# Two attentions of a two-block transformer: half of the value evictions on VectorE, another PSUM bank for x at one border, and a new order of weight splits at the ends of both attentions

## The reference, cut to what matters

```
for layer in range(2):
    h = rms_norm(x, norm_mix_pre[layer])
    h = neighbourhood_attention(...) if layer == 0 else dilated_attention(...)
    x = x + rms_norm(h, norm_mix_post[layer])
    h = rms_norm(x, norm_ffn_pre[layer])
    x = x + rms_norm(swiglu(h, ...), norm_ffn_post[layer])
```

## Time and profile before

| | us |
|---|---|
| median of 3 executions | 1777.59 |
| lowest, highest | 1774.07, 1777.84 |
| the profiled execution: its time | 1775.63 |
| the profiled execution: span from first to last instruction | 1773.8 |
| PE busy | 1760.5 (99% of the span) |
| DVE busy | 1233.4 (70%) |
| ACT busy | 1000.0 (56%) |
| POOL busy | 97.4 (5%) |

### The profile page before, as it was taken

How to read it: one execution, slowest core, us unless ns; L and a number is a source line. 1 busy time by engine, 2 the same in 40 slices (tenths; PEclk the granted TensorE clock), 3 DMA queues, 4 the chain that set the end, 5 groups by cost and what they waited for, 6 DMA issues and landing times.

```text
span 1773.8 us, 25245 instructions
## 1 busy us (share of the span) xinstructions
PE 1760.5 (99%) x9960; PEld 1504.2 (85%) x9960; DVE 1233.4 (70%) x1889; ACT 1000.0 (56%) x1588; POOL 97.4 (5%) x179
## 2 busy tenths in 40 slices
PE   8999999999999999999999999999999999999999
PEld 7878888888888788888888888888888888888887
DVE  5877774648887677557755887876487648778763
ACT  6656553555555655456544666654465536656551
POOL 0000000501110000000000110000000002100000
PEclk9999999999999999999999999999999999999999
DMA  9335565443343355535553444555365534336552
GB/s 354 132 145 188 190 226 190 186 179 143 143 154 143 144 189 202 214 143 207 188 217 127 143 149 161 214 190 214 122 222 188 217 134 167 143 143 212 189 214 75
DMA packets 45080, 314.72 MB, mean 177 GB/s; under 512 B 5008, under 2 KB 5520, under 8 KB 7968
## 3 DMA queue, kind: packets, MB, share of 16 engines
q1 hardware_dynamic: 44640, 312.54, 47.5%
q10 hardware_dynamic: 288, 0.52, 0.1%
q0 software_dynamic: 32, 0.03, 0.0%
HBM read 312.03 MB, written 1.05 MB: 176 GB/s over the span
## 4 chain that ended last, share of the span: by engine, by line
PE 97%; DVE 1%; ACT 1%; DMA 0%; issue 0%; SPq 0%; DVEq 0%
PE P L404 94%; PE P L411 1%; PE P L699 1%; DVE wl L1754 1%; DMA raw<-w_all 0%; ACT dV L1509 0%; ACT xx L1238 0%; DVE xx L1789 0%; PE P L1036 0%; PE P L605 0%; PE P L1116 0%; DVE npA L1996 0%; ACT npA L1391 0%; PE P L982 0%; DVE xs L1809 0%
## 5 line engine op out<-in xcount | busy, mean ns | idle before, releaser
L1754 DVE TENSOR_TENSOR wl<-raw,wh 128x2048 fp32r<-128x2048 f32 x287 | 656.7, 2294 | 198.8 <-ACT wh L1210 179.7
L1210 ACT ACTIVATE wh<-raw 128x2048 fp32r<-128x2048 f32 x291 | 551.6, 1900 | 189.1 <-PE P L404 167.6
L404 PE MATMUL P<-xx,wh 128*128 128x512 f32 (+2 forms) x2800 | 652.2, 385 | 1.9 <-DVE dq L2120 1.9
L404 PEld LDWEIGHTS P<-xx,wh 128*128 128x128 f32 (+1 forms) x2800 | 503.1, 188 | 102.2 <-issue 4.3
L404 PEld LDWEIGHTS P<-xx,wl 128*128 128x128 f32 x2688 | 344.3, 191 | 12.4
L404 PE MATMUL P<-xx,wl 128*128 128x256 f32 x2688 | 350.7, 283 | 0.0
L1339 ACT ACTIVATE ft<-P 128x256 f32<-128x256 f32 x240 | 90.3, 382 | 235.3 <-PE P L404 235.3
L404 PE MATMUL P<-wh,fhh 128*128 128x512 f32 x528 | 206.2, 390 | 0.0
L404 PE MATMUL P<-wh,fhl 128*128 128x512 f32 x528 | 205.5, 389 | 0.0
L404 PE MATMUL P<-wl,fhh 128*128 128x512 f32 x528 | 205.5, 389 | 0.0
L1915 DVE TENSOR_TENSOR fg<-P,ft 128x256 f32<-128x256 f32 x240 | 101.7, 424 | 123.9 <-ACT ft L1339 120.0
(11 more groups left out here) (320 smaller groups left out, 1492.6 us busy)
## 6 DMA issues: line engine op xcount, KB each, us to landing
raw<-w_all SPq DMA_DIRECT2D x289, 1024.0 KB, 4.8
nB<-rpb SPq DMA_DIRECT2D x4, 768.0 KB, 8.9
raw<-w_all SPq DMA_DIRECT2D x2, 512.0 KB, 6.9
fgb<-post SPq DMA_DIRECT2D x2, 512.0 KB, 5.5
out<-xs SPq DMA_DIRECT2D x4, 256.0 KB, 2.0
C<-cst SPq DMA_DIRECT2D x1, 769.0 KB, 8.9
xs<-x_in ACTq DMA_DIRECT2D x2, 256.0 KB, 3.6
xs<-x_in SPq DMA_DIRECT2D x1, 512.0 KB, 6.9
```

The lines of the kernel that those rows point to most:

```text
L404: return t_.on.matmul(o, l, r, start=start, stop=stop, skip_group_check=True)
L1210: a.on.activation(o, i, ACT.Copy).then_inc(*hi.up((m,)))
L1754: v.on.tensor_tensor(o, i, h.bitcast(F32), ALU.subtract).then_inc(*lo.up(m))
```

## The change

- `xbank`: for s = 3, q = 1 bank 3 instead of bank 1.
- Values of z = 1 and 2: ScalarE takes out only the banks of t = 1, and VectorE, in new `evict(z, banks)`, those of t = 0 with four `tensor_scalar` of 64 x 512. The waits of TensorE on those banks and of `values_dil` follow.
- `drb` is now all 128 rows of `rb` in permuted order; the multiplication L2122 then runs over plain views with `drb` instead of `near`/`far` views with `rb`.
- ScalarE at f = 0, z = 0 of the couples: first `side_dil(0, 0, 0)`, then `ahead` (the rounding of b0 + 15), instead of the other way round.
- End of the neighbourhood attention: VectorE makes the split of piece 13 after the last `part` instead of before `shares_na(6)`, and those of 14 and 15 no longer both before `scores_na(7)` (14 behind it, 15 after `shares_na(7)`); ScalarE does `out_na(5)` before `exps_na(7)`.
- End of the dilated attention: VectorE makes the splits of b0 + 38 and b0 + 39 no longer before `scores_dil(14)`; 38 comes behind it, 39 after `shares_dil(15)`.

```diff
@@ arena of the dilated attention
-                    ("drb", [1, S], F32)])
+                    ("drb", [128, S], F32)])
@@ xbank
-            return 6 * (1 - t) + q if s == 0 else (6, 1)[q] if s == 3 else 6 + (q if s <= 4 else t)
+            return 6 * (1 - t) + q if s == 0 else (6, 3)[q] if s == 3 else 6 + (q if s <= 4 else t)
@@ TensorE, values_dil and dil
                 t_.wait_ge(*aa.of("V", 2, 2, 3))
+                t_.wait_ge(*va.of("V", 2, 2, 1))
...
-                        held[banks[i // 2][i % 2]] = [(aa, "V", 2, z, i)]
+                        held[banks[i // 2][i % 2]] = [(aa if i >= 2 else va, "V", 2, z, i)]
@@ ScalarE, na: attend
                         probs_na(6)
+                        out_na(5)
                         exps_na(7)
-                        out_na(5)
@@ ScalarE, dil
-                    for i in ((2, 3, 0, 1) if z else range(4)):
+                    for i in (range(2, 4) if z else range(4)):
...
-                        if z == 0:
+                        if f and z == 0:
                             ahead(b0 + 12 + 3 * f + z + 2)
...
-                        if z:
+                        if z or f == 0:
                             ahead(b0 + 12 + 3 * f + z + 2)
@@ VectorE, drain
-                ahead(m + 2)
                 for i in range(16):
                     attend(i)
-                    if i % 4 == 0:
+                    if i == 0:
+                        ahead(m + 1)
+                    elif i % 4 == 0:
                         ahead(min(m + i // 4 + 2, BASE[s + 1] - 1))
@@ VectorE, na
-                    ahead(f + 5)
+                    if f < 7:
+                        ahead(f + 5)
...
+                ahead(12)
@@ VectorE, dil
-                v.on.tensor_copy(near(AD["drb"][0:1, :]), far(rb[0:1, :])).then_inc(*vx.up(("rbp", 2)))
+                v.on.tensor_copy(near(AD["drb"][:, :]), far(rb[:, :])).then_inc(*vx.up(("rbp", 2)))
...
+                def evict(z, banks):
+
+                    v.wait_ge(*mm.of("piece", b0 + 4 * z + 3))
+                    v.wait_ge(*vx.of("rr", 2))
+                    for hf in range(2):
+                        for c in range(2):
+                            p, o = slice(64 * c, 64 * c + 64), 64 * ((c + z - 1) % 2)
+                            k = v.on.tensor_scalar(AD["dV"][o:o + 64, 1 + c, 0, halfs(hf)], P[banks[hf]][p, :], rp_[p, 0:1],
+                                                   None, ALU.mult)
+                        k.then_inc(*va.up(("V", 2, z, hf)))
+
+                ahead(b0 + 9)
+                evict(1, (6, 7))
                 ahead(b0 + 13)
+                evict(2, (2, 4))
@@ VectorE, dil: part
-                    if z or j == 0:
-                        o, i, r = near(o), far(i), far(r)
-                    v.on.tensor_tensor(o, i, o, ALU.add).then_inc(*va.up(("sum", 2, f, z, j)))
+                    if z or j == 0:
+                        r = AD["drb"][:, :]
+                        v.on.tensor_tensor(near(o), far(i), near(o), ALU.add).then_inc(*va.up(("sum", 2, f, z, j)))
+                    else:
+                        v.on.tensor_tensor(o, i, o, ALU.add).then_inc(*va.up(("sum", 2, f, z, j)))
@@ VectorE, dil: couples
-                        if z == 2:
+                        if z == 2 and f < 7:
                             ahead(m + 2)
```

## The result

The changed kernel takes 1768.31 us (median of 5 runs, 1767.93 to 1768.49); the kernel before, on the same chip, 1776.10 (5 runs, 1774.07 to 1777.84). The ratio is 0.9955, with a 95% interval of [0.994, 0.9969]: faster by 0.45%, 7.8 us between the medians. The profiled execution took 1768.03 us, its span is 1766.1. Three disturbed executions of 3.5 ms and more, met in the experiments, are left out of all medians here.

A forecast was written before the change was run, and what follows sets the result against it. TensorE, busy 1760.5 of 1773.8 us, was taken as the bound; its losses, 4.3 + 2.1 + 1.0 + 0.4 = 7.8 us, came off two bases, giving 1769.0 us. Its own range was 1767.0 to 1771.0, overall 1765.5 to 1773.5.

The forecast's parts named there:

- Border of stages 2 and 3: After the last turn there, bank 3 ends TensorE's wait for xl and the half-clock stretch behind it: 4.3 us gained.
- Value evictions: At the start of the couples, sharing them with VectorE ends TensorE's wait for the sum in `dq`: 2.1 us gained.
- `drb`: In the couples, longer copy and plain views in L2122 gain 0 us, as VectorE isn't waited for there.
- End of the neighbourhood attention: Last rounds there: later splits and earlier `out_na(5)` end waits for `shares_na(6)` and `noh`: 1.0 us gained.
- End of the dilated attention: Last round there: with splits moved behind the scores, the shares end sooner: 0.4 us gained, bounds 0 and 0.5.
- The sum: Whole kernel: the gains of all places add up to 7.8 us, 4.6 with low bounds, 8.0 with high ones.
- The base: Starting time for the subtraction: profiled 1775.63 gives 1767.8, median 1777.59 gives 1769.8; the middle, 1769.0, was taken.
- The border's wait only moves: Stages 2 to 3: TensorE stops instead at the last turn's columns; gain 3.5 us, 1773.5 to 1775; chance 0.08.
- A late fetch: Dilated attention's end: fetch of piece 91, issued 11 us later, lands too late; 1781 or more; chance 0.05.
- Clock: Slow stretch at the border not in every execution, or a small term stays: 1770 to 1773; chance 0.13.

The follow-up runs named there:

- a_bank: The kernel before with only bank 3 for bank 1 at the border of stages 2 and 3: 1773.03 us, ratio 0.9983.
- f_bank1: The changed kernel with bank 1 back at the border of stages 2 and 3: 1772.09 us (7 runs), ratio 0.9974.
- h_noorder: The changed kernel with ScalarE's rounding of b0 + 15 again ahead of the first copy for `dq`: 1767.90 us in one execution.
- e_order: The kernel before with only ScalarE's new order, the first copy for `dq` ahead of the rounding: 1778.32 us in one execution.
- d_drb: The kernel before with only the 128-row `drb` copy and plain views in the multiplication L2122: 1776.31 us, ratio 1.0002.
- b_evict: The kernel before with only the value evictions shared between VectorE and ScalarE and ScalarE's new order: 1773.66 us, ratio 0.9989.
- f_look1: One more execution, on a third chip, of the changed kernel with bank 1 back at the border: 1770.75 us.
- f_look2: Another single execution, on the third chip, of the changed kernel with bank 1 back at the border: 1770.86 us.
- c_ends: The kernel before with only the new orders of splits and `out_na(5)` at the ends of both attentions: 1775.49 us, ratio 0.9998.
- g_thrice: The changed kernel with VectorE's four evictions at z = 2 made three times: 1773.25 us, ratio 0.9981.

## Why the prediction was right

The forecast was 1769.0 us and faster; it came out at 1768.31, in the range of the forecast itself.

- **Border of stages 2 and 3**, forecast 4.3 us with bounds 2.5 and 4.3: 4.32. Bank 3 alone gives it (a_bank), bank 1 alone takes it back (f_bank1). The split into wait and clock is 2.7 and 1.6 rather than 2.5 and 1.7 to 1.8. The next thing that could be late was rightly named, and is nearer than forecast: the last xl ends at 589.87 + 1.13 = 591.00, and the thirteenth matmul, the second of the pair at 591.03, starts about 0.23 later, at 591.26. That is 0.26 us of slack, not 0.42, because the first matmul begins already 0.25 before the last turn's end.
- **Value evictions**, forecast 2.1, bounds 1.5 and 2.2: 2.20. Each step holds when the 0.70 us between the time bases is added: the rounding ends at 384.33 + 0.70 = 385.03 (forecast 385.0), TensorE restarts at 387.34 + 0.70 = 388.04 (388.05). The slack is 387.34 - 387.11 = 0.23 us (0.35 forecast). The price taken for VectorE, 0.68 each, is too low: four took 3.06, about 0.76 each. It hides anyway, as it still idles 2.1 us before the split. Which half of the edit does it, the prediction didn't ask; h_noorder and e_order answer.
- **`drb`**, forecast 0: nothing in the times, 0.2 us at the transposes of one place. The copy of 128 rows takes 848 ns (d_drb), and that of one row took 848 ns in the kernel before.
- **End of the neighbourhood attention**, forecast 1.0, bounds 0.6 and 1.0: 1.19, just over the upper bound. The first half, 0.66, came out at 0.67. The second, the wait for `noh`, was sized by its marked idle time and restart, 0.33 in all; it gave 0.5.
- **End of the dilated attention**, forecast 0.4: 0.50, the upper bound. The shares come in time (0.82 for 1.18).
- **The sum**: 7.8 forecast; 8.2 in the ledger, 7.7 between the spans, 7.8 between the medians of the result.
- **The base** is where the 0.7 us of error lies. From the profiled execution the forecast is 1767.8, and 1768.03 came. I moved it up by half the distance to a median of 1777.59; with more runs the median of the kernel before is 1775.9, and the profiled execution is the better base.

**The rivals.** *The border's wait only moves* fell with the chain after. Its times had a slip: with the forecast's own two bases a gain of 3.5 us gives 1772.1 to 1774.1, not 1773.5 to 1775. *A late fetch* fell too: piece 91 is rounded at 576.02 and was at 579.40, 3.4 us sooner, exactly by what TensorE had gained up to there. *Clock* is half true. The slow stretch indeed comes in some executions and not in others: behind the same 2.5 us at the border there in the kernel before, b_evict and f_bank1, and absent in f_look1 and f_look2; behind the 1.9 us at the couples absent in the kernel before and there in c_ends. But it doesn't shrink the gain, for the kernel before has two idle stretches where it may come. Its 33 runs on one chip lie in three groups, 1773.97 to 1774.58 (9 runs), 1775.53 to 1776.32 (13) and 1777.06 to 1777.78 (11), some 1.6 us apart, the price of one slow stretch. The mean granted clock of each run bears this out: it is 1.000 in all of the lowest group, 0.999 in all of the middle one and 0.998 in nine of the highest (0.999 in two), and 1.7 us lost in 1774 are 0.001. Of the profiles, a_bank (1771.36), f_look1 and f_look2 show no slow stretch, and the kernel before (1775.63), b_evict (1773.73) and f_bank1 (1772.09), each of its kernel's middle group, one. Read so, the 33 runs have (13 + 2 x 11) / 33 = 1.1 slow stretches on average, and the profiled execution had one. That the forecast from one profile fits the medians to a tenth is luck in this term: from the lowest group to the changed kernel it is some 6 us, from the highest over 9. All ten runs of the changed kernel lie within 0.8 us.

This also explains why the parts' medians (2.8, 2.2, 0.4, -0.4) add up to 5.0 and not to 7.8: the idle terms add up, but each part alone leaves an idle stretch, and with it the chance of a slow one. Runs of equal mean clock show the parts better. At 1.000 the middle run of a_bank's lowest group is at 1771.43 and that of the kernel before at 1774.28, 2.9 us less; at 0.999 those of b_evict and c_ends are at 1773.65 and 1774.03 and that of the kernel before at 1775.85, 2.2 and 1.8 us less. The ledger has 2.7 for the wait alone, 2.2 and 1.7. So c_ends gains what was forecast, though its median hardly moves.

What remains open is the third group. With one long idle stretch left, a_bank, b_evict and f_bank1 should lie in two groups, as was expected of a_bank and f_bank1, and lie in three. Their highest runs (two, two and two) have a mean clock of 0.999 in all but one, which is that of one slow stretch, so a doubled one as in g_thrice doesn't fit, and some of the time is lost where the clock on record doesn't show it. The start of c_ends (1777.33, with two slow stretches on record and 1.8 us lost ahead of them) is such a place. Whether it is the one in those runs isn't shown: none of them was profiled, and all ten runs of the changed kernel, which starts in the same way, lie within 0.8 us, so that none of them lost as much.

No kernel here beats the changed one; h_noorder, at 1767.90 in one execution, is the same within the scatter, with 387.26 - 386.62 = 0.64 us of slack at the couples instead of 0.23.

## What to carry to other kernels

Where one engine is busy for 99% of the span, a change is priced by walking through its own waits and late starts, one by one; the terms then add up, to a tenth or two. When a wait goes, look for the next thing needed and its slack before taking the whole wait, and look for a twin of the place elsewhere in the kernel that runs without it. To end a wait at the end of a queue, pull forward what stands in the queue before the awaited piece: handing half the evictions to an idle engine did it, changing the order behind them did nothing.

## What the runs showed of the hardware

An idle stretch of TensorE of 1.9 to 2.9 us costs more than itself, but not in each execution. Behind it the granted clock was at the lower of its two levels, 1.2 instead of 2.4 GHz, for a while in some executions, at 1.4 to 1.7 us a time (once about 3 us, behind 2.9 us of idle time), and stayed up in others of the same code: f_bank1 ran seven times on one chip, with a mean clock of 1.000 in three runs and 0.999 in four. The times of the kernel before fall in groups some 1.6 us apart that go with the mean clock (1.000, 0.999, 0.998), and the changed kernel, without such an idle stretch, stays within 0.8 us over ten runs. At the start of c_ends four transposes took 1.05 us instead of 0.60 while the clock on record was 1.00: there the durations tell more than the clock row. The Trainium skill (TensorE: Matmul & The Clock Gate, section "What's actually happening") says that the observation runs freely and is not tied to the kernel's start. The two clocks of the one code of f_bank1 agree with that; no run here shows it directly.

VectorE's `tensor_tensor` of 128 x 256 with all operands in SBUF took 0.62 to 0.64 us with permuted views and 0.42 to 0.44 with plain ones, while the sum of the same size that reads PSUM took 0.42 with permuted views too. Evicting 64 x 512 from PSUM with a multiplication took 0.75 us on VectorE (mean of 8 in the kernel after) and 0.68 on ScalarE (mean of 16 in the kernel before).
